# Compressed-key scores of the first attention, each placed behind one dense product of the value tile's second half

## What is computed

```
s_c = einsum("bqgrd,bngd->bgrqn", q * HEAD_DIM**-0.5, kc) - slopes * (t - cmp_center)
p_c = masked_softmax(s_c, cmp_end <= t)
o_c = einsum("bgrqn,bngd->bqgrd", p_c, vc)
```

## Time and profile before

| what | us |
|---|---|
| median of three runs | 754.82 |
| lowest and highest | 753.05, 755.27 |
| the profiled execution | 755.52 |
| its span, first to last instruction | 753.7 |
| TensorE busy (matmul) | 733.9 |
| VectorE busy | 539.1 |
| ScalarE busy | 377.4 |

### The profile page before, as it was taken

The page is one execution under the profiler, slowest core; times in us unless marked ns, Lnnn a source line. Parts: engine busy times, 40 slices in busy tenths (PEclk is TensorE's granted clock), DMA queues, the critical chain, the costliest instruction groups (busy, mean ns, idle before and its releaser), DMA issues.

```text
span 753.7 us, 13081 instructions
## 1 busy us (share of the span) xinstructions
PE 733.9 (97%) x5264; PEld 676.4 (90%) x5264; DVE 539.1 (72%) x926; ACT 377.4 (50%) x542; POOL 51.2 (7%) x72
## 2 busy tenths in 40 slices
PE   5999999999999999999999999999999999999996
PEld 4999986789999999998999999999988998998995
DVE  6798787586677777756758988785967876555554
ACT  7433767756334333445545346664634544444442
POOL 1950000000000000000333000000000000000000
PEclk9999989999999999999999999999999999999999
DMA  8636411288778878843355456555632675644611
GB/s 334 226 120 230 162 57 57 73 335 327 287 295 319 313 300 306 306 142 112 114 179 177 168 173 235 205 202 195 238 154 87 249 257 190 215 161 180 223 57 56
DMA packets 27021, 151.08 MB, mean 200 GB/s; under 512 B 3128, under 2 KB 7836, under 8 KB 9564
## 3 DMA queue, kind: packets, MB, share of 16 engines
q1 hardware_dynamic: 22620, 124.81, 46.0%
q10 hardware_dynamic: 3456, 25.17, 8.3%
q0 software_dynamic: 896, 0.43, 0.3%
HBM read 148.92 MB, written 1.05 MB: 199 GB/s over the span
## 4 chain that ended last, share of the span: by engine, by line
PE 90%; DVE 6%; issue 1%; ACT 1%; DMA 1%; SPq 0%; DVEq 0%; ACTq 0%
PE ps L467 27%; PE ps L468 26%; PE ps L469 26%; PE ps L574 2%; PE ps L773 2%; PE ps L598 1%; DMA raw<-wts 1%; DVE w_lo L1644 1%; PE ps L1023 1%; DVE rows_ga L1783 1%; PE ps L1009 0%; PE ps L608 0%; PE ps L686 0%; PE ps L999 0%; PE ps L969 0%
## 5 line engine op out<-in xcount | busy, mean ns | idle before, releaser
L1644 DVE TENSOR_TENSOR w_lo<-raw,w_hi 128x2048 fp32r<-128x2048 f32 x106 | 239.9, 2268 | 109.3 <-ACT w_hi L1202 109.2
L467 PE MATMUL ps<-h_hi,w_hi 128*128 128x256 f32 (+2 forms) x1000 | 284.9, 285 | 0.6 <-DVE h_lo L1696 0.6
L468 PE MATMUL ps<-h_lo,w_hi 128*128 128x256 f32 (+2 forms) x1000 | 282.8, 283 | 0.0
L469 PE MATMUL ps<-h_hi,w_lo 128*128 128x256 f32 (+2 forms) x1000 | 282.8, 283 | 0.0
L1202 ACT CAST w_hi<-raw 128x2048 fp32r<-128x2048 f32 x106 | 198.8, 1887 | 47.3 <-PE ps L469 46.5
L467 PEld LDWEIGHTS ps<-h_hi,w_hi 128*128 128x128 f32 (+2 forms) x1000 | 190.2, 190 | 3.3 <-issue 2.1
L468 PEld LDWEIGHTS ps<-h_lo,w_hi 128*128 128x128 f32 (+2 forms) x1000 | 190.2, 190 | 1.2
L469 PEld LDWEIGHTS ps<-h_hi,w_lo 128*128 128x128 f32 (+2 forms) x1000 | 190.2, 190 | 0.3
L467 PE MATMUL ps<-w_hi,mix_hi 128*128 128x512 f32 x248 | 97.4, 393 | 1.2 <-DVE small L1783 0.8
L468 PE MATMUL ps<-w_lo,mix_hi 128*128 128x512 f32 x248 | 96.8, 390 | 0.0
L469 PE MATMUL ps<-w_hi,mix_lo 128*128 128x512 f32 x248 | 96.5, 389 | 0.0
(11 more groups left out here) (307 smaller groups left out, 899.0 us busy)
## 6 DMA issues: line engine op xcount, KB each, us to landing
raw<-wts SPq DMA_DIRECT2D x109, 1024.0 KB, 4.8
ada<-w_ada ACTq DMA_DIRECT2D x24, 1024.0 KB, 5.4
alibi<-wts SPq DMA_DIRECT2D x2, 1024.0 KB, 7.0
fa_whole<-wts SPq DMA_DIRECT2D x2, 1024.0 KB, 6.1
resid<-x SPq DMA_DIRECT2D x2, 512.0 KB, 4.2
raw<-wts SPq DMA_DIRECT2D x2, 512.0 KB, 6.7
rows_ga<-rows_wide SPq DMA_DIRECT2D x1, 1024.0 KB, 6.9
out<-resid SPq DMA_DIRECT2D x4, 256.0 KB, 2.0
```

What stands on the lines that cost most here:

```text
L467: nc.tensor.matmul(o, lh, rh, start=start, stop=False)
L468: nc.tensor.matmul(o, lh, rl, start=False, stop=False)
L469: return nc.tensor.matmul(o, ll, rh, start=False, stop=stop)
L1644: V.tensor_tensor(w_lo[:, s % RING, 0:w], raw[:, n_of[name] % RAW, 0:w], w_hi[:, s % RING, 0:w].bitcast(F32), ALU.subtract).then_inc(w_rea ...
```

## The change

The helper `token_tile` is no longer used for `vs`; its body is written out. The first half of the tokens is as before. The wait for `vblk_ready` and `cmp2_sb` now stands between the halves. In the second half each of the 24 products is followed by one of the 24 scores. The tile's signal `pe_tile` sits on the last dense product, `sc_ps` on the last score. Products, operands, banks and their number are unchanged.

```diff
-            token_tile(*own_bank("vs"), h_hi, h_lo, 0, T, T).then_inc(pe_tile, 1)
-
-            pe.wait_ge(vblk_ready, NQ)
-            pe.wait_ge(cmp2_sb, 2)
-            for m in range(2):
-                for h in range(NQ):
+            def compressed_scores(n0, n1):
+
+                for n in range(n0, n1):
+                    m, h = n // NQ, n % NQ
                     _, b, _ = head_at(h)
                     g = h // 3
...
-            i.then_inc(sc_ps, 1)
+                return i
+
+            slot, bank = own_bank("vs")
+            wh, wl = w3(slot, DC)
+            for k in range(DC):
+                mm3(ps[:, bank, 0:T], h_hi[:, k, 0:P], h_lo[:, k, 0:P], wh[:, k, :], wl[:, k, :], k == 0, k == DC - 1)
+            pe.wait_ge(vblk_ready, NQ)
+            pe.wait_ge(cmp2_sb, 2)
+            for k in range(DC):
+                o, lh, ll = ps[:, bank, T:2 * T], h_hi[:, k, P:T], h_lo[:, k, P:T]
+                nc.tensor.matmul(o, lh, wh[:, k, :], start=k == 0, stop=False)
+                compressed_scores(3 * k, 3 * k + 1)
+                nc.tensor.matmul(o, lh, wl[:, k, :], start=False, stop=False)
+                compressed_scores(3 * k + 1, 3 * k + 2)
+                i = nc.tensor.matmul(o, ll, wh[:, k, :], start=False, stop=k == DC - 1)
+                j = compressed_scores(3 * k + 2, 3 * k + 3)
+            i.then_inc(pe_tile, 1)
+            j.then_inc(sc_ps, 1)
```

## The result

The changed kernel took 770.8 us (median of 5 runs, 769.72 to 771.56), the kernel before 753.32 (median of 5, 753.0 to 755.27): ratio 1.0221, with a 95% interval of 1.0208 to 1.0235. The change makes the kernel 17.5 us slower. The forecast was 770.

The account below looks back on a forecast made before the run. TensorE was taken as the bound, busy 733.9 of 753.7 us. Units of 21.5 us plus "vw" at 8.3 make 29.8 against 14.86, +14.9; with the profiled 755.5 that is 770.4, for a median 770 us, range 760 to 776.

Parts of the forecast that it names:

- Not hidden at the switch: In the 24 units, switching between 128 and 64 rows exposes weight loads: 0.60 us per unit at the high clock.
- the 0.10 for 64 rows in place of 8: Added to the 0.52 us unit price for a score's longer weight loads, giving the upper end of 0.62 us.
- The clock: In the units it falls 5 us after scores begin, making units 1.05 us; returns after 5.78 us of "vw".
- The early wait: The wait for value blocks and keys comes 24 products earlier, at 86.0 us, costing 0.1 us at most.
- what waits behind: After "vw", the keys' last weights are ready at 117.5, before TensorE comes at 120.3: no new wait.
- The base of the sum: Second half of "vs" through "vw": 29.8 us replaces the profiled 14.86, adding 14.9 us to the kernel.
- against 14.86: The profiled time from the first product of the second half of "vs" to the end of "vw", subtracted from 29.8.
- The first rival: In the units, score loads run under dense neighbours and the clock holds: 0.23 us per unit, 752 us; chance 8%.
- Loads stay hidden: Same case as the first rival: score loads hidden at the row switch, clock holding, -2.8 us; chance 8%.
- Drains, but the clock holds: Units cost 0.60 us at the row switches but stay at 2.4 GHz: +5.3 us, 760 us; chance 11%.

Follow-up runs that it names:

- the bursts: The changed kernel with the scores behind every third or every sixth dense product, three or six at a time: 764.64 and 758.72 us.
- e_pad_inter: The changed kernel with keys zero-padded so each score uses all 128 rows, queries of two heads as stationary operand: 755.88 us.
- e_fill2: The changed kernel with two more dense products per unit, whose result is not read: 769.5 us.
- e_pair_opp: The changed kernel regrouped as two dense products, then two scores on opposite halves of the rows, twelve times: 761.92 us.
- e_fill3: The changed kernel with three more dense products per unit, whose result is not read: 771.14 us.
- e_before_again: The kernel before, unchanged, profiled a second time: 753.22 us.
- e_bursts6: The changed kernel with six scores behind every six dense products, four times: 758.72 us.
- the two padded kernels: Keys zero-padded so scores use all 128 rows, in the changed kernel (755.88 us) and in the kernel before, scores in a row (757.79 us).
- e_alt: The kernel before with the heads in the block of 24 scores alternating between the halves of the rows: 752.31 us.
- e_joined_alt: The kernel before with alternating heads and the second head pair's scores moved directly ahead of the block: 752.12 us, ratio 0.9985.

## Why the prediction was right, and where not

- **Not hidden at the switch: right.** In all 24 units the score's weights start to load only 0.31 us after the dense product (0.51 at the low level), where between dense products it is 0.12. The reasoning gave 0.52 + 0.10 = 0.62 us per unit, of which 0.60 was taken; it was 0.636. The term that was short is the 0.10 for 64 rows in place of 8, which stands in truth for 0.12. It was put down to longer loads; the bursts show that 0.109 us of a lone score is its second pass, which starts that much after the first.
- **The clock: right that it falls.** Fall at 5 us, measured 4.66 after the first score; 1.05 us per unit at the low level, measured 1.05; back after 5.8 us of "vw", measured 3.57. The 5 us are in part luck: they are twice the 2.46 us of a block that in 36 of 42 executions doesn't lose the clock. The units end at 21.5 us after the start, measured 21.9 (86.87 to 108.75), "vw" takes 7.4 us for 8.3, and the whole is 29.3 for 29.8.
- **The early wait and what waits behind: right.** The first unit starts 0.12 us after the last product of the first half (86.75, 86.87), so the wait costs nothing. TensorE meets no new wait for the late keys.
- **The base of the sum: wrong, and the time came out by luck.** The step "against 14.86" took the profiled execution of before for the kernel. I read its clock at 0.50 for 6.8 us as how the kernel runs, and compared with a stretch that is 3 us too long for 36 of 42 executions. So +14.9 should have been +17.5 up to the turn, and +17.0 over the rest of the execution. The kernel before was put at 754.8, the median of its first three runs, 1.5 us above the 753.32 of the five. The two errors have opposite signs; that is why 770 came within 1 us of 770.8. The first rival rested on the same step: by its own prices, 2.9 + 24 x 0.23 + 5.8 = 14.2 us, it was worth 0.6 us against the usual 14.81, for there was no clock to win back.
- **The rivals.** "Loads stay hidden" would have been 0.23 us per unit. Even without any switch (e_pad_inter) it is 0.34, so padding doesn't make this kernel faster in this way. "Drains, but the clock holds" is what e_fill2 shows, at +9.1 us and not the +5.3 that the wrong base gave.
- **Slips that change nothing.** The 8 in the clock's line of the earlier trace rows is in the sixth slice, not the fifth. A 64-row product follows a dense one nine times in the trace of before and not seven, at 0.21 us each time. In the first rival the keys' weights would be ready 10.0 us after the units' end at 91.6, at 101.6 and so before TensorE comes at 101.8; the 0.7 us that it gives back aren't there.
- **The rule of the Trainium skill** ("TensorE: Matmul & The Clock Gate", Part 2), that weights are loaded ahead under running matmuls: the trace agrees between products of the same rows (0.12 us), and for opposite halves of 64 rows (two scores in e_pair_opp take no longer than one). At a switch between 128 and 64 rows it doesn't. Part 1 of that page ties the low clock to idle time; here no instruction of TensorE waited for another engine in the units, and yet the clock fell in the profile (the mean clock is 0.984 to 0.986 in all 5 executions of the change).

## What to carry to other kernels

Count the changes between products that use all 128 rows and products that use 64, for each pair of them costs about 0.3 us in which no product starts; small products belong together, with the halves of the rows alternating, or padded with zeros to the full rows if they must be spread. Spreading small products among dense ones is no cure for the clock by itself: in this kernel it fell where one dense product stood between two switches (the change) and held where three or four did (e_fill2, e_fill3), at 9 us for the placing. And before a stretch at the low clock is taken for the cost of a place in the code, read more than one execution: here the mean clock of each run told that it wasn't the rule, and only a second profile told where the time went.

## What was not expected of the hardware

- Two passes on opposite halves of the rows run beside each other although they follow one another in the program (0.76 us for 0.97), even six passes apart: the 48 passes of the long block take 3.02 us in e_before_again, where 0.109 each would make 5.2. Two on the same half take 0.109 us each.
- The clock held with one score in 0.87 us among three dense products (e_fill2) and with one in 0.34 us on full rows (e_pad_inter), and fell with six scores among six dense products (e_bursts6), in one profile of each. No simple count of products puts these in order; what decides it is open.
- The start differs between executions. In the 14 profiles TensorE's first instruction lies between 7.5 and 9.1 us. The dense products, which begin at 12.7 to 14.3 us, are 0.12 us apart almost from the first in eleven of them, but 0.21 apart, as at the low level, until 16.8 to 17.6 us in e_fill2 and the two padded kernels. From the first dense product to the gate tile it is 63.8 us in before, its repeat, e_alt, e_joined_alt and the changed kernel, and 65.2 to 65.7 in those three. Part of what the padded kernels lose may lie there; whether the padding causes it wasn't tried.
